# A fourth staging place for expert weights, taken from the descriptor scratch, and another order of loads on SP

## The reference

```python
N_EXPERTS, TOP_K, D_EXPERT = 32, 4, 1024      # D_MODEL = 1024, T = 256 tokens

logits = (ht @ w_router + b_router).astype(jnp.float32)
top_vals, top_idx = lax.top_k(logits, TOP_K)
gates = jax.nn.softmax(top_vals, axis=-1)
...
gu = xblk @ w_gate_up[e] + b_gate_up[e]       # 1024 x 2048 per expert: 8 MB
gate = jnp.minimum(gu[:, :D_EXPERT], 7.0)
up = jnp.clip(gu[:, D_EXPERT:], -7.0, 7.0)
act = gate * jax.nn.sigmoid(1.702 * gate) * (up + 1)
return act @ w_down[e] + b_down[e]            # 1024 x 1024 per expert: 4 MB
```

## Time and profile before

| | |
|---|---|
| median of 3 runs | 1493.42 us (1492.33 to 1495.0) |
| span of the profiled execution | 1490.6 us |
| PE busy | 1415.9 us (95%) |
| POOL busy | 416.3 us (28%) |
| bytes moved | 480.73 MB, mean 323 GB/s |
| granted PE clock, mean | 0.989 |

### The profile page before, as it was taken

The page is one execution under the profiler, slowest core; times in us unless marked ns, Lnnn a source line. Parts: engine busy times, 40 slices in busy tenths (PEclk is TensorE's granted clock), DMA queues, the critical chain, the costliest instruction groups (busy, mean ns, idle before and its releaser), DMA issues.

```text
span 1490.6 us, 20373 instructions
## 1 busy us (share of the span) xinstructions
PE 1415.9 (95%) x7344; PEld 781.2 (52%) x7345; DVE 650.3 (44%) x1102; ACT 248.9 (17%) x424; POOL 416.3 (28%) x432
## 2 busy tenths in 40 slices
PE   8999999999989999999999999999999999999995
PEld 7668867999976664343333343343333334333332
DVE  3134735677654553344443344444444434333333
ACT  1222113444423420010001010010000001000001
POOL 3000011222216233334433435444443444200000
PEclk9999999999999999999999999999999999999998
DMA  8433344455533878999996999999999999999995
GB/s 276 147 136 113 113 134 149 170 196 174 177 126 135 300 283 358 429 427 427 429 427 276 429 429 427 427 427 428 429 427 427 427 428 429 427 427 429 427 429 226
DMA packets 77413, 480.73 MB, mean 323 GB/s; under 512 B 7019, under 2 KB 31272, under 8 KB 52808
## 3 DMA queue, kind: packets, MB, share of 16 engines
q1 hardware_dynamic: 74046, 477.45, 78.6%
q10 hardware_dynamic: 3338, 2.88, 0.6%
HBM read 479.26 MB, written 1.05 MB: 322 GB/s over the span
## 4 chain that ended last, share of the span: by engine, by line
PE 51%; DMA 39%; POOL 5%; DVE 3%; issue 1%; ACT 1%; SPq 0%; POOLq 0%; ACTq 0%; DVEq 0%
DMA stage<-in_w_gate_up 28%; PE bank L2127 10%; PE bank L1866 8%; PE bank L1614 8%; DMA ring<-in_w_gate_up 7%; PE bank L1624 6%; PE bank L2203 5%; POOL ring L599 5%; PE bank L1878 4%; PE bank L1798 2%; DMA ring_b<-in_w_gate_up 2%; DMA ring_b<-in_w_down 2%; PE bank L2108 1%; PE bank L1675 1%; PE bank L2162 1%
## 5 line engine op out<-in xcount | busy, mean ns | idle before, releaser
L599 POOL COPY ring<-stage 128x1024 f32<-128x1024 f32 x300 | 310.3, 1080 | 443.7 <-DMA stage<-in_w_gate_up 359.7
L2127 PE MATMUL bank<-ring,x_T 128*64 128x512 f32 x1584 | 368.0, 610 | 38.1 <-POOL ring L599 31.3
L2127 PEld LDWEIGHTS bank<-ring,x_T 128*64 128x64 f32 x1584 | 111.0, 140 | 272.6 <-issue 205.9
L2203 PE MATMUL bank<-ring_b,act_T 128*64 128x512 f32 x1056 | 236.1, 596 | 1.1 <-ACT act_T L872 0.5
L1494 DVE TENSOR_TENSOR h<-h,bank 128x512 f32<-128x512 f32 x128 | 82.2, 683 | 243.9 <-PE bank L2162 243.9
L2203 PEld LDWEIGHTS bank<-ring_b,act_T 128*64 128x64 f32 x1056 | 72.0, 137 | 147.9 <-issue 125.7
L2127 PE MATMUL bank<-ring_b,x_T 128*64 128x512 f32 x528 | 120.6, 598 | 2.3 <-DMA ring_b<-in_w_gate_up 2.3
L1470 DVE SCALAR_TENSOR_TENSOR y_lo<-bank,slot_gate,y_hi 128x512 fp32r<-128x512 f32 x33 | 24.8, 751 | 194.8 <-ACT y_hi L852 194.8
L866 ACT ACTIVATE sig<-bias_raw 128x512 f32<-128x512 f32 x33 | 20.8, 629 | 509.5 <-DVE bias_raw L1500 509.5
L1866 PE MATMUL bank<-h_hi,ff_hi 128*128 128x256 f32 x352 | 99.8, 284 | 1.9 <-POOL h_lo L531 1.4
L1866 PE MATMUL bank<-h_lo,ff_hi 128*128 128x256 f32 x352 | 99.6, 283 | 0.0
(11 more groups left out here) (435 smaller groups left out, 1609.4 us busy)
## 6 DMA issues: line engine op xcount, KB each, us to landing
stage<-in_w_gate_up SPq DMA_DIRECT2D x75, 2048.0 KB, 25.0
ring_b<-in_w_down SPq DMA_DIRECT2D x64, 2048.0 KB, 23.0
ring_b<-in_w_gate_up SPq DMA_DIRECT2D x32, 2048.0 KB, 20.9
ring<-in_w_gate_up SPq DMA_DIRECT2D x21, 2048.0 KB, 25.5
ring<-in_w_in SPq DMA_DIRECT2D x22, 1024.0 KB, 7.2
ring<-in_w_ffn_in SPq DMA_DIRECT2D x22, 1024.0 KB, 5.1
ring<-in_w_ffn_out SPq DMA_DIRECT2D x11, 1024.0 KB, 4.7
ring<-in_w_out SPq DMA_DIRECT2D x8, 1024.0 KB, 6.1
```

The lines of the kernel that those rows point to most:

```text
L599: ins = pool.tensor_copy(pair_slot(g, pair)[:, cols], t.stage[:, pair, cols])
L2127: ins = pe.matmul(banks[n][rows, :], t.x_T[:, c, :], job_slot(g, c)[:, c0:c0 + 512], start=False, stop=(c == GU - 1), skip_group_check=True)
L2203: ins = pe.matmul(banks[4][rows, :], t.act_T[:, k, SLOTS * (c // 2):SLOTS * (c // 2) + SLOTS], job_slot(g, GU + c)[:, c0:c0 + 512], start= ...
```

## The change

The reserve for descriptors is cut from its default to 256 bytes, and the space becomes `stage_b`, one more staging place of 2 MB, for pair 3. All four pairs of experts 1 to 25 are staged and copied by POOL; the direct load `next_last_pair` is gone. Pair 3 of expert 1 is loaded into `stage_b` while the second part's chunks are loaded, behind the sixth of them. POOL's copy of pair 3 waits for `gu_full` (`pair_used`). In the loop SP issues staged pairs 0 and 1 of m+2, the down halves of m+1, staged pairs 2 and 3 of m+2. The last six experts load in the same order as before.

```diff
-AHEAD = PAIRS - 1
+def stage_place(g, pair):
+    return g.t.stage[:, pair, :] if pair < PAIRS - 1 else g.t.stage_b[:]
+
+def pair_used(g, job, pair):
+    if pair == PAIRS - 1:
+        return g.s.gu_full, job * 2 + 2
+    return g.s.gu_used, job * (PAIRS - 1) + (pair + 1)
...
         load(g.n_second + n, src, shape)
+        if n == RING - 1:
+            load_stage(1, PAIRS - 1)
...
     def load_stage(e, pair):
-        sp.dma_start(t.stage[:, pair, :], gate_up[e, pair]).then_inc(s.staged[pair], 16)
+        sp.dma_start(stage_place(g, pair), gate_up[e, pair]).then_inc(s.staged[pair], 16)
...
-    def next_last_pair(m, last):
-        sp.wait_ge(s.gu_full, last * 2 + 2)
-        load_gu(m + 1, PAIRS - 1)
...
     sp.wait_ge(s.jobs_ready, 1)
     last = last_job(0)
-    next_stage(0, 0)
-    next_stage(0, 1)
-    next_last_pair(0, last)
-    next_stage(0, 2)
+    for pair in range(PAIRS):
+        next_stage(0, pair)
     for h in range(2):
         next_down(0, last, h)
     with sp.Fori(1, STAGED - 2) as m:
         last = last_job(m)
-        next_last_pair(m, last)
         next_stage(m, 0)
+        next_stage(m, 1)
         for h in range(2):
             next_down(m, last, h)
-        next_stage(m, 1)
         next_stage(m, 2)
+        next_stage(m, 3)
     last = last_job(STAGED - 2)
-    next_last_pair(STAGED - 2, last)
...
-        for pair in range(AHEAD):
+        for pair in range(PAIRS):
             pool.wait_ge(s.staged[pair], m * 16 + 16)
-            pool.wait_ge(s.gu_used, last * AHEAD + (pair + 1))
+            pool.wait_ge(*pair_used(g, last, pair))
...
-        if m is None or pair == PAIRS - 1:
+        if m is None:
             pe.wait_ge(*expert_landed(g, e, 2 * pair))
+            pe.sem_inc(s.in_place[pair], 16)
         else:
             pe.wait_ge(s.in_place[pair], e * 16 + 16)
...
-        self.stage = new("stage", [AHEAD, 2 * CW])
+        self.stage = new("stage", [PAIRS - 1, 2 * CW])
...
+        self.stage_b = new("stage_b", [2 * CW])
...
-    nc = bacc.Bacc("TRN2", target_bir_lowering=False, num_devices=1)
+    nc = bacc.Bacc("TRN2", target_bir_lowering=False, num_devices=1, dynamic_dma_scratch_size=256)
```

More of the change, by code:

```diff
@@ L356, in sync_program, with load_gu, load_stage, load_down @@
     load_ffn(FF_STEPS - 1, "o", 0, FF_STEPS - 1)
+    gate_up = w["w_gate_up_2"].rearrange("e (c p i) n -> e c p (i n)", p=P, i=2)
+    down = w["w_down_2"].rearrange("e (h p i) n -> e h p (i n)", h=2, p=P)
+    def load_gu(e, pair):
+        sp.dma_start(pair_slot(g, pair), gate_up[e, pair]).then_inc(s.job_landed(2 * pair), 16)
+    def load_stage(e, pair):
+        sp.dma_start(stage_place(g, pair), gate_up[e, pair]).then_inc(s.staged[pair], 16)
+    def load_down(e, h):
+        sp.dma_start(pair_slot(g, PAIRS + h), down[e, h]).then_inc(s.job_landed(GU + 2 * h), 16)
     former = [("o", 3), ("g", 2), ("a", 1), ("o", 2), ("g", 1), ("o", 1)]
@@ L365, in sync_program @@
         load(g.n_second + n, src, shape)
[L369 to L375, removed]
-        sp.dma_start(t.stage[:, pair, :], gate_up[e, pair]).then_inc(s.staged[pair], 16)
-    def load_down(e, h):
-        sp.dma_start(pair_slot(g, PAIRS + h), down[e, h]).then_inc(s.job_landed(GU + 2 * h), 16)
+        if n == RING - 1:
+            load_stage(1, PAIRS - 1)
     sp.wait_ge(*g.r2.filled("pm1"))
@@ L397, in sync_program @@
     load_down(0, 0)
-    for pair in range(1, AHEAD):
+    for pair in range(1, PAIRS - 1):
         load_stage(1, pair)
@@ L441, in sync_program @@
         last = last_job(m)
-        for pair in range(AHEAD):
-            sp.wait_ge(s.gu_used, last * AHEAD + (pair + 1))
+        for pair in range(PAIRS):
+            sp.wait_ge(*pair_used(g, last, pair))
             sp.dma_start(pair_slot(g, pair), gate_up[m + 1, pair]).then_inc(s.in_place[pair], 16)
-        next_last_pair(m, last)
         for h in range(2):
@@ L598, in gpsimd_program @@
                 cols = slice(1024 * q, 1024 * q + 1024)
-                ins = pool.tensor_copy(pair_slot(g, pair)[:, cols], t.stage[:, pair, cols])
+                ins = pool.tensor_copy(pair_slot(g, pair)[:, cols], stage_place(g, pair)[:, cols])
             ins.then_inc(s.in_place[pair], 16)
@@ L2115, in gate_up @@
             pe.wait_ge(s.x_ready, nth(m, o, 2, 2))
-        if m is None or pair == PAIRS - 1:
+        if m is None:
             pe.wait_ge(*expert_landed(g, e, 2 * pair))
+            pe.sem_inc(s.in_place[pair], 16)
         else:
             pe.wait_ge(s.in_place[pair], e * 16 + 16)
-        if m is None and pair < AHEAD:
-            pe.sem_inc(s.in_place[pair], 16)
         for n in range(2):
@@ L2397, in __init__ @@
         self.out_ready = new("out_ready")
-        self.staged = [new(f"staged{n}") for n in range(AHEAD)]
+        self.staged = [new(f"staged{n}") for n in range(PAIRS)]
         self.place_free = new("place_free")
-        self.in_place = [new(f"in_place{n}") for n in range(AHEAD)]
+        self.in_place = [new(f"in_place{n}") for n in range(PAIRS)]
         self.out_ready_act = new("out_ready_act")
```

## The result

| | before | after |
|---|---|---|
| median of the runs side by side, us | 1494.21 (1492.33 to 1498.94) | 1485.61 (1483.24 to 1488.27) |
| the profiled execution, us | 1492.33 (from its span) | 1488.27 |
| its span, us | 1490.6 | 1486.5 |

The ratio is 0.9936, with a 95% interval of 0.9916 to 0.9956: 9.6 us faster (6.6 to 12.6). Of before it was the fastest: all other runs on record lie 1.7 us above their spans, and so does 1492.33.

A forecast was written before the change was run, and what follows sets the result against it. DMA was taken as the bound, through the bytes left after it last stands still. Terms -10.2 - 4.9 + 5.4 = -9.7, plus 0.2 contention, gave -9.5: span 1481.1, median 1483.9 us, range 1480.5 to 1488.3.

The forecast's parts named there:

- H: The prediction's reading: end is when DMA last stands still, plus bytes to come; place and order count only through holes.
- hole: DMA idle time while SP waits for job 9's down product; two staged loads cover 9.8 of 15.2 us: 5.4 us.
- The bound and the count: Whole kernel: DMA's remaining transfers, 4.903 us each, counted from when it last stood still, set the end, within a microsecond.
- First full moment, 2.4 us: Around the experts' start: transfers up to expert 8's second down half end at 784.3, not 786.7; job 9 2.4 us earlier.
- rival B: The first full moment gives nothing, DMA being partly idle at 545 to 600 us anyway: 1486.1 to 1488.3 us; chance 0.11.
- Second full moment, -10.2 - 4.9 + 5.4: At expert 8's two jobs: loading resumes 10.2 us earlier, one transfer fewer left saves 4.9, a hole costs 5.4.
- PE's waits: Before, 2.05 us at a gate/up pair; now ahead of the down product's two halves, 1.8 and 1.4 us a job.
- rival D: Two waits around the down product slow PE's clock, deciding from 3.7 us a job: slower, 1516 us; chance 0.05.
- Rival C: The place fills no earlier, since pair 3 is freed 4.1 us later, after POOL's copy: no change, 1493.4 us; chance 0.04.
- Contention, +0.2: POOL's added copies lengthen two VectorE operations with two SBUF inputs in jobs 1 and 9: 0 to 2.2 us, taken as 0.2.
- The scratch, 0: Cutting the descriptor reserve loses nothing, as the program issues no transfer from POOL: 0 us.
- SP then stands at d2.0: 595.20 as before: Ahead of expert 2's first down load, SP waits for job 1's down product until 595.20 us, unchanged by the change.

The follow-up runs named there:

- scratch alone: Kernel before with only the descriptor scratch cut to 256 bytes, places, order and copies unchanged: 1494.09 us, ratio 1.0002.
- order alone: Kernel before, its three places kept, loop order changed: staged pairs 0 and 1, direct load of pair 3, down halves, staged pair 2: 1489.14 us, ratio 0.9963.
- after, again: The changed kernel unaltered, measured once more beside the kernel before: 1484.58 us, ratio 0.9938.
- three ahead of down: Changed kernel with staged pairs 0, 1 and 2 issued ahead of the down halves, pair 3 behind: 1482.42 us, ratio 0.9926 against before.
- one ahead of down: Changed kernel with only staged pair 0 issued ahead of the down halves, pairs 1 to 3 behind: 1486.19 us, ratio 0.9956 against before.
- s1.3 late: Changed kernel with expert 1's staged pair 3 loaded behind its pair 2, at 530.35 us instead of 437.59: 1482.69 us, ratio 0.9928 against before.
- more copies: Changed kernel with 12 further small GpSimd copies per expert behind the fourth pair's copy: 1484.16 us, ratio 0.9932 against before.

## Why the prediction held, step by step

The count of H beside the traces (for before and the scratch alone the first transfer is g9.3; these two and the order alone have 135 left). The last column takes the lag out:

| kernel | job 1 starts | issue of s10.0 | hole | end by the count | last byte in the trace | from job 1 to the last byte |
|---|---|---|---|---|---|---|
| before | 572.08 | 806.93 (g9.3) | 0 | 1471.6 | 1470.7 | 898.6 |
| scratch alone | 571.87 | 807.44 (g9.3) | 0 | 1472.1 | 1471.1 | 899.2 |
| after | 577.01 | 801.04 | 5.4 | 1466.2 | 1464.9 | 887.9 |
| after, again | 574.39 | 798.34 | 5.4 | 1463.5 | 1462.3 | 887.9 |
| three ahead of down | 569.96 | 798.02 | 0.5 | 1458.3 | 1457.5 | 887.5 |
| one ahead of down | 571.50 | 795.63 | 10.3 | 1465.7 | 1464.5 | 893.0 |
| order alone | 574.54 | 805.10 | 0.5 | 1470.3 | 1469.7 | 895.2 |
| s1.3 late | 571.58 | 795.10 | 5.4 | 1460.3 | 1459.0 | 887.4 |
| more copies | 571.78 | 795.45 | 5.4 | 1460.6 | 1459.3 | 887.5 |

- **The bound and the count: right.** In nine traces the count is 0.6 to 1.3 us above the last byte, though the holes run from 0 to 10.3 us and the issue moves by 12 us. Behind the second full moment nothing but bytes and that hole sets the end. One sentence of the prediction is too narrow: DMA stands still not only when every place is full. In the hole SP stands at d9.0, while the place of s10.2 is free: the order with three loads ahead fills it.
- **First full moment, 2.4 us: right, against rival B.** The lag is taken out by measuring from job 1's start: s10.0 follows it after 224.0, 224.0, 223.5 and 223.7 us in the four traces with the change's order of the loop. The prediction makes it 796.7 - 572.08 = 224.6, B 227.0. That s1.3 costs nothing at 437 us held; that it has to be there did not matter (s1.3 late).
- **Second full moment, -10.2 - 4.9 + 5.4: right.** In the two traces with the change's order and without a lag s10.0 is 11.5 to 11.8 us ahead of 806.93, and d9.0 comes 15.2 us behind it in all seven traces that start with s10.0. The two order experiments with four places move the hole to 0.5 and 10.3. The larger hole moves the end with it: measured from job 1 the last byte comes 5.1 to 5.6 us later. The smaller one, in its one trace, does not move it: 887.5 is the changed kernel's figure, because s10.0 leaves 228.1 us after job 1, 4.1 to 4.6 later than in the change's order, where H had 1.3.
- **PE's waits: moved as predicted.** From 960 to 1260 us, ten jobs, PE waits for no gate/up pair any more and for the down halves only (busy, mean ns of one, idle before):

```profile
L2205 PE MATMUL bank<-ring_b,act_T 128*64 128x512 f32 x320 | 77.5, 632 | 24.2 <-DMA ring_b<-in_w_down 24.2
```

That is 2.4 us of waiting a job for the expected 3.2. Most of the rest went into slower matmuls: 77.5 / 10 = 7.75 us a job where the two halves take 7.0 to 7.1 without a wait, some 0.7 more. (The mean of 632 ns can't be multiplied by 32: 32 matmuls of 592 ns end within 7.1 us, so they overlap.) It is not the same in every job; two of the ten:

```profile
1000.37 3.65 PE L2205 MATMUL bank<-ring_b,act_T 128*64 128x512 f32 x16 [1.76 <-DMA ring_b<-in_w_down]
...
1029.78 8.78 PE L2205 MATMUL bank<-ring_b,act_T 128*64 128x512 f32 x32 [1.75 <-DMA ring_b<-in_w_down]
```

In seven jobs PE waits at either half, 1.2 to 1.8 us and then 1.2, and each half takes 3.65; in three it waits once, 1.8 us, and the product takes 8.78. So rival D's mechanism is there, but far below the 3.7 us from which it decides, and it eats time in which PE would have waited: the granted clock over 820 to 1300 us is 0.99, DMA's share 1.01. In the order alone, with one wait a job, it is 0.9 us a job over the same 300 us (4.53 for 3.65), and 3.0 us in the one job where it counted.

- **Rival C: out.** s10.0 left at 795 to 801, not 806.
- **Contention, +0.2: measured as nothing**, by L1505 in jobs 1 and 9 (0.85 and 0.84 us, before 0.88 and 0.87). The Trainium skill, GPSIMD Engine Reference, Key points, says that GpSimd contends with VectorE's instructions that have two SBUF inputs; the longest L1505 and L1511 of the changed kernel, 1006 and 1126 ns beside medians of 693 and 692, agree, and by the rule alone the 2.2 us end of the sum could have been due. With more than twice the change's copies nothing of that is seen in the time.
- **The scratch, 0: right**, by a run of its own.
- **What was missing: the clock ahead of the experts.** The sum took job 1's start as fixed. It starts between 569.96 and 577.01 in these traces, and the whole course behind it shifts along. The step at fault is "SP then stands at d2.0: 595.20 as before", 4.95 us too early for the profiled execution; from there the steps hold. The 5.4 us of 1486.5 over 1481.1 are this lag of 4.95, less 1.25 by which the rest up to the last byte went better than forecast (1464.9 beside 1461.2), and 1.7 of the tail: the end is 21.6 us behind the last byte, not 19.9, since the last down product fell into a stretch with a granted clock of 0.75 (1465 to 1470) and took 8.78 us, where 7.0 are usual. The median hardly suffers, probably because before's runs have such lags too: 17 of them range from 1490.96 to 1497.52, and in them a granted clock lower by 0.001 in the mean goes with about 1 us more (0.991 with a span of 1489.3, 0.985 with 1495.4). That these are lags ahead of the experts is argued; the two traces with before's order start job 1 at 572.08 and 571.87. Measured from job 1's start the change brings the last byte forward by 10.7 to 11.8 us (898.6 and 899.2 to 887.4 to 887.9), 1 to 2 us more than the sum. So the agreement of 9.6 with 9.5 is closer than the sum deserves, and in part luck; the interval is 3 us wide on either side.

What stays open: why the clock falls ahead of the experts in one execution and not in the next (the instructions are the same), and whether the changed kernel meets it more often than that before. The runs differ too little to tell. The early load of s1.3 is not the cause by itself: the order alone, without it, has a lag of 2.5 us, and three ahead, one ahead and more copies have it and no lag. The standstill ahead of the first full moment (share 0.31 from 550 to 560 us in the changed kernel) is closed where s1.3 is loaded late (1.01), but only by a load that was otherwise done before; filling it with a further one would need a fifth place and was not tried.

## What to carry to other kernels

Where one resource is full to the end, a change is worth what it does at the last moment when that resource stood still: the time at which it starts again, and the bytes left; count transfers from there. A prefetch place is worth something only if the issue order lets it fill such a moment, so try the order by itself and the place by itself: here the order alone gave 5.5 us, the place with one load ahead, as before, 6.6, and both 9.6, less than their sum, since they fill the same standstill. A second load ahead of the blocking wait moved the last byte by 5.1 to 5.6 us, measured from job 1; a third, in its one trace, did not move it. When a profiled execution misses a good forecast, look for the place where it came off, and measure the rest from there.

## What the runs showed of the hardware that was not expected

- After a wait of 3.13 us 16 matmuls took 6.64 us (3.65 is usual, 5.32 after 2.05 us): the slow clock behind a wait can cost as much as the wait. But after waits of the same length they took anything from 3.65 to 6.64 us, and after a first wait of 1.2 to 1.8 us the two halves of a down product took 7.3 us in seven of ten jobs and 8.78 in three. In the mean over ten jobs a single wait cost 0.9 us a job (order alone), two shorter ones 0.7 (changed kernel).
- PE can run near the slow level for several microseconds with hardly a wait in front (0.41 us ahead of the row at 545.63), in some executions only. The scatter of this kernel, some 6 us, goes along with the mean granted clock.
- One core's DMA holds 428 GB/s for 640 us, unmoved by 130 us more of GpSimd's copies. The Trainium skill, Perfetto Trace Analysis, Roofline, gives some 435 GB/s for a core that is alone on its memory; the trace is within 2% of it.
